# The front of a two-block transformer kernel: scale and shift chunks in turn, one w_in column early, x and ctx behind the first four weight tiles

## What is computed

```python
mod = (silu(c) @ w_ada + b_ada)[:, None, :]        # 6 x 2048 columns; mod_c the same from c_ctx
sh_a, sc_a, gt_a, sh_f, sc_f, gt_f = split(mod, 6)
h  = rms_norm(x,   g_attn) * (1 + sc_a)  + sh_a
hc = rms_norm(ctx, g_attn) * (1 + csc_a) + csh_a
pl = split(h  @ w_in)     # 4928 columns: inputs of four kinds of attention (NA, GQA, MLA, DIFF)
pc = split(hc @ w_in)     # of these, the columns that the context needs
```

## Time and profile before

| what | value |
|---|---|
| median of three runs | 3047.54 us |
| the profiled execution | 3046.9 us, span 3045.1 us |
| front: first ada unit to last shift added | 45.5 to 145.1 us |
| columns 0 to 4 of the mix: VectorE's first `lo` of ML_Q to its first of GQ_Q | 145.24 to 343.48 us |
| VectorE's first `lo` behind the mix (MLA) | 530.7 us |

### The profile page before, as it was taken

How to read it: one execution, slowest core, us unless ns; L and a number is a source line. 1 busy time by engine, 2 the same in 40 slices (tenths; PEclk the granted TensorE clock), 3 DMA queues, 4 the chain that set the end, 5 groups by cost and what they waited for, 6 DMA issues and landing times.

```text
span 3045.1 us, 33828 instructions
## 1 busy us (share of the span) xinstructions
PE 2837.6 (93%) x12623; PEld 2272.2 (75%) x12623; DVE 1748.4 (57%) x2063; ACT 1153.0 (38%) x1487; POOL 220.7 (7%) x223
## 2 busy tenths in 40 slices
PE   2889989898899999999979998999999999999997
PEld 0367767566778888888867886788787888888886
DVE  1479886366645555555574445544554565565555
ACT  2122222243444444434443444444444444444433
POOL 1215160000100000000051000000000000000000
PEclk9799999979999999999989999999999999999998
DMA  7979976114656555555545552355545555565552
GB/s 270 336 278 304 318 256 234 56 42 168 199 170 199 187 193 192 193 189 184 192 138 194 193 193 69 139 193 193 193 155 178 192 186 186 189 197 181 192 192 96
DMA packets 285721, 579.31 MB, mean 190 GB/s; under 512 B 11225, under 2 KB 14008, under 8 KB 283080
## 3 DMA queue, kind: packets, MB, share of 16 engines
q1 hardware_dynamic: 280592, 557.50, 55.1%
q0 software_dynamic: 3088, 20.65, 1.9%
q10 hardware_dynamic: 1960, 0.09, 0.0%
HBM read 572.93 MB, written 5.28 MB: 190 GB/s over the span
## 4 chain that ended last, share of the span: by engine, by line
issue 63%; PE 17%; DVE 11%; DVEq 2%; DMA 2%; ACT 1%; ACTq 1%; POOL 1%; POOLq 0%
DVE proj_ctx L1365 6%; PE bank L332 4%; PE bank L334 4%; PE bank L333 4%; DVE w_lo L328 2%; DMA w_raw<-in_w_ada 2%; DVEq L1364 2%; PE bank L558 2%; ACTq L1116 1%; PE bank L1646 1%; PE bank L591 1%; ACT probs L665 1%; PE bank L575 0%; POOL x_one L1932 0%; POOL h_mix L1936 0%
## 5 line engine op out<-in xcount | busy, mean ns | idle before, releaser
L328 DVE TENSOR_TENSOR w_lo<-w_raw,w_hi 128x1024 fp32r<-128x1024 f32 (+2 forms) x864 | 1047.9, 1233 | 705.0 <-ACT w_hi L320 693.0
L320 ACT ACTIVATE w_hi<-w_raw 128x1024 fp32r<-128x1024 f32 (+2 forms) x864 | 899.2, 1054 | 1321.1 <-PE bank L334 1117.4
L332 PE MATMUL bank<-w_hi,xa_hi 128*128 128x512 f32 (+1 forms) x2304 | 908.1, 394 | 43.6 <-DVE w_lo L328 42.2
L333 PE MATMUL bank<-w_lo,xa_hi 128*128 128x512 f32 (+1 forms) x2304 | 899.9, 391 | 0.0
L334 PE MATMUL bank<-w_hi,xa_lo 128*128 128x512 f32 (+1 forms) x2304 | 899.7, 390 | 0.0
L332 PEld LDWEIGHTS bank<-w_hi,xa_hi 128*128 128x128 f32 x2304 | 436.5, 189 | 152.9 <-DVE w_lo L328 31.8
L334 PEld LDWEIGHTS bank<-w_hi,xa_lo 128*128 128x128 f32 x2304 | 436.1, 189 | 91.0
L333 PEld LDWEIGHTS bank<-w_lo,xa_hi 128*128 128x128 f32 x2304 | 436.7, 190 | 87.8
L332 PE MATMUL bank<-w_hi,ffn_act_hi 128*128 128x512 f32 x864 | 338.9, 392 | 7.9 <-DVE w_lo L328 7.9
L333 PE MATMUL bank<-w_lo,ffn_act_hi 128*128 128x512 f32 x864 | 338.2, 391 | 0.0
L334 PE MATMUL bank<-w_hi,ffn_act_lo 128*128 128x512 f32 x864 | 338.1, 391 | 0.0
(11 more groups left out here) (270 smaller groups left out, 1716.0 us busy)
## 6 DMA issues: line engine op xcount, KB each, us to landing
w_raw<-in_w_in SPq DMA_DIRECT2D x116, 1024.0 KB, 5.0
w_raw<-in_w_ada SPq DMA_DIRECT2D x96, 1024.0 KB, 5.5
w_raw<-in_w_up SPq DMA_DIRECT2D x64, 1024.0 KB, 5.2
w_raw<-in_w_down SPq DMA_DIRECT2D x64, 1024.0 KB, 5.1
w_raw<-in_ffn_wg SPq DMA_DIRECT2D x44, 1024.0 KB, 5.1
w_raw<-in_ffn_wu SPq DMA_DIRECT2D x44, 1024.0 KB, 5.1
w_raw<-in_ffn_wd SPq DMA_DIRECT2D x44, 1024.0 KB, 5.1
w_raw<-in_w_out SPq DMA_DIRECT2D x32, 1024.0 KB, 5.1
```

The source lines that it names most:

```text
L320: act.activation(whi[:, slot, ks, 0:w], raw[:, q, ks, 0:w], ACT.Copy)\
L328: dve.tensor_tensor(wlo[:, slot, ks, 0:w], raw[:, q, ks, 0:w], whi[:, slot, ks, 0:w].bitcast(F32), ALU.subtract).then_inc(sem("lo_made"), 1)
L332: pe.matmul(out, xh, wh, start=first, stop=False)
L333: pe.matmul(out, xh, wl, start=False, stop=False)
```

## The change

Scale and shift chunks alternate: chunk c has column block c // 2 of the scale (c even) or of the shift (c odd). So group g of h is ready after chunk 2g + 1. The column DF_V of w_in becomes column 0 and goes into the front as "win" units 0 to 3: one tile behind each of chunks 2, 4 and 6 and one at the end (`FRONT`, 36 tiles). Its `hi` and `lo` are `early_hi` and `early_lo`; its matmuls, four row blocks of 12, stand as `early_piece` behind the four units of chunks 3, 5 and 7 and, for the fourth, behind the front. They keep banks 0 to 3; the ada sums have bank 4 alone, the spread rows banks 5 and 6, and a turn of h has bank 7 (group 3: 7 and 4). `turn_h_pe(g)` stands in chunk 2g + 2 behind the third unit. The band matmuls move into chunk 1, 16 behind each unit. The table `na_rpb` comes in by rows and is turned by one transpose on TensorE; Silu stands ahead of it. x and ctx are issued behind the first four weight tiles. In the mix nine columns are left, and `per` gives 2, 2, 2, 3 late units to ML_Q, ML_KV, DF_Q, DF_K instead of 1, 2, 1, 2 (and DF_V's 3); from GQ_Q on it is unchanged. The SBUF places of some tables move.

```diff
-WIN = [(ML_Q, 512, None), (ML_KV, 320, CX_ML), (DF_Q, 512, None), (DF_K, 512, CX_DK), (DF_V, 512, CX_DV),
+WIN = [(DF_V, 512, CX_DV), (ML_Q, 512, None), (ML_KV, 320, CX_ML), (DF_Q, 512, None), (DF_K, 512, CX_DK),
...
+def front_loads():
+
+    loads = []
+    for c in range(N_ADA_1):
+        loads += [("ada", c, q) for q in range(4)]
+        if c % 2 == 0 and c:
+            loads.append(("win", 0, c // 2 - 1))
+    return loads + [("win", 0, 3)]
...
-    per = [1, 2, 1, 2, 3, 1, 2, 1, 3, 0]
+    per = [0, 2, 2, 2, 3, 1, 2, 1, 3, 0]
...
+        def early_piece(pe, k, j):
+
+            if j == 0:
+                if k == 0:
+                    pe.wait_ge(sem("na_bias_made"), 1)
+                pe.wait_ge(sem("h_lo"), 4 * k + 4)
+            if j % 2 == 0:
+                pe.wait_ge(sem("early_lo"), 2 * k + j // 2 + 1)
+            for tk in range(4):
+                X, c = (XA, XB)[tk // 2], slice((tk % 2) * P, (tk % 2) * P + P)
+                m = mm3(pe, ps[tk][:, :], X[0][:, 4 * k + j, c], X[1][:, 4 * k + j, c], whi[:, k % 2, j, :],
+                        wlo[:, k % 2, j, :], k == 0 and j == 0, k == 3 and j == 3)
+            m.then_inc(sem("early_used"), 1)
...
         def turn_h_pe(pe, g):
             for i in range(4):
                 pe.wait_ge(sem("h_ready"), 4 * g + i + 1)
-                wait(pe, "h_lo", 4 * g + i - 3)
+                wait(pe, "h_lo", 4 * g + i - (g == 3 and i >= 2))
...
-            for i in range(4):
-                sp.dma_start(xin[:, i, :], (x_v, ctx_v)[i // 2][:, i % 2, :]).then_inc(sem(f"x_loaded{i // 2}"), 16)
...
+            for n, (kind, c, q) in enumerate(FRONT):
+                front_read(sp, n)
+                src = w_ada_v[:, q, :, ada_cols(c)] if kind == "ada" else w_in_v[:, q, :, WIN[0][0]:WIN[0][0] + NCH]
+                sp.dma_start(raw[:, n % 4, :, :], src).then_inc(sem(f"landed{n % 4}"), 16)
+                if n == 3:
+                    for i in range(4):
+                        sp.dma_start(xin[:, i, :], (x_v, ctx_v)[i // 2][:, i % 2, :])\
+                            .then_inc(sem(f"x_loaded{i // 2}"), 16)
+                    sp.wait_ge(sem("memsets"), 4)
+                if kind == "ada" and q == 3:
+                    b_piece(c)
...
-                        act.dma_start(narpb[p:p + 31, h * 7:h * 7 + 7], t["na_rpb"][0, h, 4:11, :].rearrange("r m -> m r"))\
-                            .then_inc(sem("na_tables_loaded"), 16)
+            act.wait_ge(sem("c_loaded"), 32)
+            act.activation(csig[:, :], crow[:, :], ACT.Silu).then_inc(sem("c_silu"), 1)
+
+            act.wait_ge(sem("memsets"), 2)
+            for h in range(4):
+                for p in (0, 32):
+                    act.dma_start(rpb[h * 7:h * 7 + 7, p:p + 31], t["na_rpb"][0, h, 4:11, :])\
+                        .then_inc(sem("na_tables_loaded"), 16)
...
             for c in range(N_ADA_1):
                 if c:
                     take(c - 1)
+                if c >= 2 and c % 2 == 0:
+                    turn_h_dve(dve, c // 2 - 1)
                 take_sums(c)
...
                 if c == 1:
                     make_na_bias()
...
+                if c >= 2 and c % 2 == 0:
+                    early_lo(dve, c // 2 - 1)
             take(N_ADA_1 - 1)
+            turn_h_dve(dve, 3)
+            early_lo(dve, 3)
...
             for c in range(N_ADA_1):
-                wait(pe, "ada_rows", c - 1)
+                wait(pe, "ada_rows", c)
                 for q in range(4):
-                    ada_unit(c, q, 2 + c % 2)
+                    ada_unit(c, q)
+                    if c == 1:
+                        if q == 0:
+                            pe.wait_ge(sem("na_rpb_lo"), 1)
+                        for j in range(16 * q, 16 * q + 16):
+                            m = pe.matmul(ps[q][:, (j % 16) * 28:(j % 16) * 28 + 28], bandr[:, 63 - j:191 - j],
+                                          narpbr[:, :], start=True, stop=True)
+                        m.then_inc(sem("na_bands"), 1)
+                    if c >= 3 and c % 2:
+                        early_piece(pe, c // 2 - 1, q)
                     if q == 1 and c:
                         spread_row(c - 1)
...
+                    if q == 2 and c >= 2 and c % 2 == 0:
+                        turn_h_pe(pe, c // 2 - 1)
...
             spread_row(N_ADA_1 - 1)
+            turn_h_pe(pe, 3)
+            for j in range(4):
+                early_piece(pe, 3, j)
```

More of the change, by code:

```diff
@@ L157, in build @@
         scale_g = at("scale_g", [P, 2, NCH], F32, 164)
[L158 to L163, removed]
+        nab_1 = at("na_bias_early", [P, 4, 2, 256], F32, 168)
+        band = at("na_band", [63, 191], F32, 176)
+        bandr = at("na_band_r", [63, 191], F32R, 177)
+        rpb = at("na_rpb_rows", [28, 64], F32, 179)
+        namask = at("na_mask", [P, 64], F32, 179.25)
+        narpbr = at("na_rpb_hi_lo", [63, 28], F32R, 179.5)
         xin = at("x_in", [P, 4, D], F32, 128)
@@ L349, in unit, with early_hi, early_lo, turn_bank @@
                     m.then_inc(sem("unit_used"), 1 + (2 * follow if j == k - 1 else 0))
+        def early_hi(act, k):
+            q = landed_front(act, ("win", 0, k))
+            for h in range(2):
+                wait(act, "early_used", 4 * (k - 2) + 2 * h + 2)
+                act.activation(whi[:, k % 2, 2 * h:2 * h + 2, :], raw[:, q, 2 * h:2 * h + 2, :], ACT.Copy)\
+                    .then_inc(sem("early_hi"), 1)
+        def early_lo(dve, k):
+            q = FRONT.index(("win", 0, k)) % 4
+            for h in range(2):
+                dve.wait_ge(sem("early_hi"), 2 * k + h + 1)
+                dve.tensor_tensor(wlo[:, k % 2, 2 * h:2 * h + 2, :], raw[:, q, 2 * h:2 * h + 2, :],
+                                  whi[:, k % 2, 2 * h:2 * h + 2, :].bitcast(F32), ALU.subtract)\
+                    .then_inc(sem("early_lo"), 1)
+        def early_piece(pe, k, j):
[10 more added lines that the diff above has]
+            m.then_inc(sem("early_used"), 1)
+        def turn_bank(g, i):
+            return 4 if g == 3 and i % 2 else 7
         def turn_h_pe(pe, g):
@@ L1135, in _ @@
             m.then_inc(sem("x_scaled"), 1)
-            for g in range(3):
+            for g in range(4):
                 turn_h_act(act, g)
+                early_hi(act, g)
             def win_copy(c):
                 col, w, cx = WIN[c]
-                used(act, U_MIX + LAST["win", c] + 1)
+                if c == 0:
+                    act.wait_ge(sem("early_used"), 16)
+                    act.wait_ge(sem("na_bias_stored"), 16)
+                else:
+                    used(act, U_MIX + LAST["win", c] + 1)
                 b = 4 * (c % 2)
@@ L1415, in _ @@
                 u, c = U_MIX + n, MIX[n][1]
+                if i == 1:
+                    win_copy(0)
                 if i >= 2 and MIX[W[i - 2]][2] == 3:
@@ L1421, in _ @@
                 lo(dve, u // 4, u % 4, w=WIN[c][1], slot=i % 2)
[L1422 to L1423 removed]
+                if i == 0:
+                    dve.wait_ge(sem("na_bias_stored"), 16)
                 for k in range(FOLLOW[i]):
@@ L1864, in _ @@
             pool.drain().then_inc(sem("mla_normed"), 1)
-            for c, col in ((2, DF_Q), (3, DF_K)):
+            for c, col in ((3, DF_Q), (4, DF_K)):
                 copied(c)
```

136 lines of the change are left out of this document (61 added, 75 removed).

## The result

| | before | after |
|---|---|---|
| median of five runs each | 3047.54 us (3045.22 to 3050.37) | 3060.51 us (3053.52 to 3065.70) |
| ratio, 95% interval | | 1.0039 (1.0025 to 1.0054) |
| profiled execution, its span | 3046.9, 3045.1 | 3053.5, 3051.7 |
| VectorE starts GQ_Q | 343.48 | 359.27 |
| VectorE starts MLA, behind the whole mix | 551.95 | 572.00 |

The account below looks back on a forecast made before the run. The front was taken as limited by ScalarE's queue, transfers and h's last turn, the mix by VectorE. GQ_Q starts at 350.7 instead of 343.48, 7.2 us later; 3046.9 + 7.2 = 3054.1 us, range 3036 to 3072.

Parts of the forecast that it names:

- M: VectorE's first subtraction of the MLA inputs, behind the whole mix, 551.95 us before; 7.2 us later by the forecast.
- the tail: Everything behind the mix, to the end of the span: same code, so no difference in time was forecast.
- T1: Front, when VectorE takes the first shift: forecast at 61 us, or 58 if the bias were free.
- T7: Front, when VectorE takes the fourth shift, behind chunk 7: forecast at 160.1 us.
- D: Rival at the start: small transfers still hold ScalarE's queue or x comes later; first shift 66 to 70, 3059 to 3063; chance 0.14.
- the same 8 MB was down at 32: Start: the same 8 MB is queued as before, so ctx lands at 32 us and the fifth tile at 34.6.
- E: Rival: shorter start, bands and burst starts at full clock, first shift 55 to 57; up to 15 us less, 3040; chance 0.16.
- The pair of chunks: Front from c=2, even chunk with one-bank turn plus odd chunk with early pieces: 33.7 us a pair, tiles 24.7.
- Rival C: Front: clock stays at 1.2 GHz in odd chunks, 13 us more each; 3067 for one, 3093 for three; chance 0.10.
- The mix: Late columns up to GQ_Q: VectorE sets the pace; moving DF_V saves it only 4 `lo`, 9.4 us; GQ_Q at 350.7.
- B: Rival: TensorE sets the mix, so moving DF_V's matmuls gives 18.9 us, 3028; chance 0.10.
- From there on all is equal: From GQ_Q on: order of units, multiplications and banks are the same in both kernels, so no difference.

Follow-up runs that it names:

- start_xfirst: The kernel before with only the new start (Silu first, na_rpb by rows and one transpose), x and ctx still ahead of the weight tiles: 3018.55 us, ratio 0.9899.
- after_xfirst: The changed kernel with x and ctx issued ahead of the first four weight tiles: 3057.4 us, ratio 1.0046.
- after_norope: The changed kernel with GpSimd's rotation of column DF_K left out, output lacking it: one execution, 3061.64 us; GQ_Q's column 23.9 us.
- alt_only: The changed kernel without the early column: DF_V back in the mix with the old late-unit counts, turns through one bank: 3039.47 us, ratio 0.9966.
- alt_turns3: The changed kernel without the early column and with turns of h through banks 7, 5, 6, 7: 3024.76 us, ratio 0.9924.
- turns3: The changed kernel with each group of h turned through banks 7, 5, 6, 7, early column kept: 3038.55 us, ratio 0.9957.
- after_halfmul: The changed kernel with two of VectorE's four multiplications of each late ada unit left out: one execution, 3009.99 us.
- before_halfmul: The kernel before with two of VectorE's four multiplications of each late ada unit left out: one execution, 3013.42 us.

## Why the prediction came out as it did

The forecast was slower by 7, with 3036 to 3072 as its range; 13 slower was measured. The sign and the mechanism were right: the start gives, the one-bank turn takes, VectorE sets the mix. The size was right by luck, since two errors nearly cancel: the part up to M was short by 12.9 us (7.2 forecast, 20.05 measured), and the tail, taken as equal, was 13.5 shorter in the profiled execution. In the two profiled executions that left 6.6 us between the kernels; the medians are 13 us apart.

| step | forecast | measured | error carried |
|---|---|---|---|
| Silu | by 6 | 2.83 | |
| ctx's squares, fifth tile's matmul | 32, 34.6 | 36.4, 39.2 | |
| first shift taken, T1 | 61 | 67.46 | +6.5 |
| fourth shift taken, T7 | 160.1 | 168.82 | +8.7 |
| `win_copy(0)` | 182.2 | 191.51 | +9.3 |
| first `lo` of GQ_Q | 350.7 | 359.27 | +8.6 |
| GQ_Q's column | as before, 23.9 | 28.0 | +12.7 |
| M against before | +7.2 | +20.05 | +12.9 |

**The start, T1.** Right: Silu, the first tile at 8.45, and that small rows are not held (D's half with the queue was wrong; the 5 us kept for it weren't needed for that). The Trainium skill, "DMA: Bandwidth & Descriptors", section "Issuing engines are not separate DMA queues", says that transfers from all engines interleave on the same DMA engines. The trace agrees: the rows were turned on TensorE at 27.61 us, before x was there (30.74), whose transfers SyncE had begun to issue at 4.75.

Mis-sized were two terms. By "the same 8 MB was down at 32" ctx was due at 32 and the fifth tile's matmul at 34.6; they came 4 and 4.6 us later. For ctx the 13 us for which SyncE's queue was held in the middle of issuing x are a likely cause. For the fifth tile they are not the main one: with x first, issued in 2.1 us with ctx, it came at 37.2 (`start_xfirst`) and 38.0 (`after_xfirst`), and in before the four tiles behind x and ctx held the queue for 16.7 us and the traffic was down by 33 us all the same. Why the fifth tile needs 3 us more than the sum stays open. And 16 band matmuls were taken at 2.6 us. The rows of TensorE in after:

```profile
41.09 3.59 PE L1741 MATMUL bank<-na_rpb_hi_lo,na_band_r 63*128 63x28 f32 x16
44.61 1.94 PE L1719 MATMUL bank<-w_raw,c_stationary 128*32 128x512 f32 x8
46.47 3.59 PE L1741 MATMUL bank<-na_rpb_hi_lo,na_band_r 63*128 63x28 f32 x16
49.99 3.78 PE L1728 MATMUL bank<-ada_rows,row_pick 128*128 128x512 f32 x4
...
55.57 1.97 PE L1741 MATMUL bank<-na_rpb_hi_lo,na_band_r 63*128 63x28 f32 x16
...
58.46 3.09 PE L1741 MATMUL bank<-na_rpb_hi_lo,na_band_r 63*128 63x28 f32 x16
```

Three of the four groups took more than the 16 x 0.18 = 2.9 us of half clock; the units beside the first two took 1.94, not 1.06, and the spread 3.78, not 2.0. Chunk 1 was 20.5 us long instead of 16.7. (The granted clock reads 1.00 in the window of 41 to 45 us, but a unit of 1.94 us is as long as the one at 76.66, where it reads 0.56.) Part of the +6.5 is this execution's: in after_norope, with the same front, the fourth group took 1.96 us and not 3.09, and the first shift was taken at 64.96.

```profile
57.11 1.96 PE L1741 MATMUL bank<-na_rpb_hi_lo,na_band_r 63*128 63x28 f32 x16
```

Six profiled kernels with x behind the tiles run alike up to there. In three the fourth group took 3.0 to 3.1 us and T1 is 66.7 to 67.5 (after, alt_only, alt_turns3); in three it took 1.95 to 1.96 and T1 is 63.8 to 65.0 (turns3, after_halfmul, after_norope). What selects the case is open. D gave 66 to 70 for x late; `after_xfirst`, where x was early, has 64.34, as the quick three have. So x late isn't shown to be the reason. E, with the bands at full clock and T1 at 55 to 57, is out.

**The pair of chunks.** 33.7 forecast; 34.96 and 33.55 measured, and 32.85 to the fourth take. That is the best term of the sum, by two errors: the early pieces were taken to run 4.5 us at half clock and did so for 1.8 (81.27 to 83.06; 0.52 up to 83 us, 1.00 after it), while from the third round on the transposes of a turn ran at half clock (2.60 a round instead of 2.15), which no step had priced. Rival C, a clock that stays at half in the odd chunks, is out: 1.00 from 83 to 92 us. The Trainium skill, "TensorE: Matmul & The Clock Gate", section "What's actually happening", says that the array is throttled by default and that activity releases it. The trace agrees in kind, by the same 0.52 and 1.00; what it cost lay in the turn more than in the bursts.

**The mix.** From `win_copy(0)` to GQ_Q 168.5 us forecast, 167.8 measured; the steps were 29.4, 39.5, 43.7 and 55.2 for ML_Q to DF_K, where the sum has 30.4, 39.2, 43.0 and 55.9. B is out: in the mix of after TensorE works 138.7 of 167.8 us. That the moved column gives VectorE only four `lo` was right, and the table of experiments bears it out (2.0 and 2.8 us returned from the last take to M).

**"From there on all is equal"** failed, by 4.1 us. The order of units from GQ_Q on is equal, but GpSimd's is not: it is one column behind, and with DF_V gone from that place its rotation of DF_K falls beside GQ_Q. The prediction had the prices in hand: the earlier trace rows give `w_lo` 1287 ns in the mean and 2.35 us for two undisturbed. It didn't ask whose work would now lie beside what. In before the same price was paid beside DF_V, where the rotation of DF_K lay (301.3 to 315.8 us).

**The tail.** It was taken as equal code and so as equal time. Windows of one and the same stretch, 84 us behind M, first before, then after:

```profile
636.00:663.30 27.30, 26.83 (x79) 16.93 (x78) 14.33 (x35) 8.71 (x26) 1.64 (x3) 0.50 0.00 1
```

```profile
656.05:683.35 27.30, 22.87 (x111) 14.39 (x110) 20.48 (x49) 12.24 (x39) 2.67 (x5) 0.94 0.00 1
```

In before the granted clock is 0.50 for all of 27.3 us, and 79 matmuls' records end where after gets through 111. after_norope, with after's front, has the long stretch at 0.50 as well, a tail of 2493.0 us and 3061.64 in all.

## What to carry to other kernels

Before moving matmuls to a place where TensorE idles, ask what the engine that sets the pace gets back: here four subtractions of 2.35 us, for a front that grew by 20 to 23 us. A group of transposes that goes PE, ACT, DVE through one bank costs its whole round trip for each tile; two more banks, free at that moment, were worth 20 us at M with the early column and 17 without, each counted from the first take. Where a step says "from here on all is equal", check it for every engine, the idle-looking one too, and for the neighbours that its instructions will have.

## What the hardware showed that was not expected

- **The same code behind M took 2479.7 to 2493.4 us** over twelve profiled kernels, and the three longest tails (before, turns3 and after_norope: 2493.2, 2493.4, 2493.0) are those with 27.3 us at 0.50 some 84 us behind M. Tails with 23.9 us at 0.50 earlier on took 2490.3 and 2490.4 (alt_turns3, before_halfmul). after and after_norope show both cases for one and the same front. The rest lie near 2487.4 (four) and 2480 (three). What selects the case stays open: it was seen, not controlled. Executions of one kernel differ too: turns3's seven lie from 3028.67 to 3044.03 us. The 13.7 us are more than the 7.2 that were forecast, and so M, not the total, was what the experiments were compared by.
- **A transfer can hold the queue that issues it for long, SyncE's too:** x's two 1024 KB transfers behind four weight tiles took 13.0 us to issue, and in before four weight tiles behind x and ctx took 16.7. Eight transfers of rows of 31 numbers took 3.86 us, where the same table by single numbers had taken 39.5.
- **GpSimd's operations on 128x256 lengthened VectorE's of 128x512 from 751 to 919 ns** in the mean of a column, and `w_lo` from 1210 to 1410, with GpSimd busy 16.5 of 28.0 us.
- **The clock fell within a turn, where TensorE is never idle for 2 us:** with gaps of 1.5 to 1.9 us between groups of four transposes, the third and fourth took 1.09 us instead of 0.63, and the granted clock from 72 to 78 us was 0.56 in the mean.
